# Block sums of the down projections chained by DMA, their issues spread out, and a stage's first weights loaded before a residual

## The reference

```python
def conv_ffn(h, w_up, w_dw, b_dw, w_down):
    u = depthwise_conv(h @ w_up, w_dw) + b_dw
    gate, val = jnp.split(u, 2, axis=-1)
    return (jax.nn.silu(gate) * val) @ w_down
...
    for i in range(DEPTH):
        m_lat = jnp.split((jax.nn.silu(c) @ w_mod[i] + b_mod[i])[:, None, :], 6, axis=-1)
        ...
        x_lat = x_lat + m_lat[2] * rmsnorm(y_lat, g_post_mix[i])
        h = modulate(rmsnorm(x_lat, g_pre_ffn[i]), m_lat[3], m_lat[4])
        x_lat = x_lat + m_lat[5] * rmsnorm(
            conv_ffn(h, ffn_w_up[i], ffn_w_dw[i], ffn_b_dw[i], ffn_w_down[i]), g_post_ffn[i])
```

## Time and profile before

| | |
|---|---|
| median of 3 runs | 2653.39 us (2651.99 to 2656.15) |
| the profiled execution | 2649.16 us, span 2647.1 us |
| PE busy | 2469.2 us (93%), 11028 matmuls |
| DVE busy | 1907.1 us (72%) |
| ACT busy | 1261.9 us (48%) |
| POOL busy | 1065.3 us (40%) |
| POOL's DMA queue | 145.77 MB, 27.9% of the 16 engines' span |
| SP's DMA queue | 248.46 MB, 26.2% |

### The profile page before, as it was taken

How to read it: one execution, slowest core, us unless ns; L and a number is a source line. 1 busy time by engine, 2 the same in 40 slices (tenths; PEclk the granted TensorE clock), 3 DMA queues, 4 the chain that set the end, 5 groups by cost and what they waited for, 6 DMA issues and landing times.

```text
span 2647.1 us, 32056 instructions
## 1 busy us (share of the span) xinstructions
PE 2469.2 (93%) x11028; PEld 1974.5 (75%) x11028; DVE 1907.1 (72%) x2537; ACT 1261.9 (48%) x2062; POOL 1065.3 (40%) x765
## 2 busy tenths in 40 slices
PE   8989998979899999988999799999899999889997
PEld 4878887768687787767788587657677787667886
DVE  5467675657558999865655679997479999566556
ACT  3356564546544555444554342235446555444542
POOL 0077667773034566644101221111435665542002
PEclk9999998989999999998999899999899999899999
DMA  6057666753521565454975456666414555458755
GB/s 253 26 162 174 158 162 151 188 155 83 187 96 68 148 172 154 123 125 106 271 232 175 141 155 136 127 142 148 123 53 146 160 150 151 100 125 237 244 175 175
DMA packets 170645, 400.93 MB, mean 151 GB/s; under 512 B 14977, under 2 KB 16257, under 8 KB 170497
## 3 DMA queue, kind: packets, MB, share of 16 engines
q0 software_dynamic: 59040, 145.77, 27.9%
q1 hardware_dynamic: 109872, 248.46, 26.2%
q10 hardware_dynamic: 1584, 4.85, 0.5%
HBM read 331.91 MB, written 170.92 MB: 190 GB/s over the span
## 4 chain that ended last, share of the span: by engine, by line
PE 35%; DVE 20%; DMA 18%; POOL 13%; issue 11%; ACT 2%; SPq 0%; POOLq 0%; ACTq 0%; DVEq 0%
DMA weight_sums<-units 14%; PE psum L2259 10%; PE psum L2261 10%; PE psum L2260 10%; DVE weights_f32r L1980 8%; POOL low L885 3%; DMA set<-mod_w 2%; POOL set L833 2%; DVE low L1957 2%; DVE low L1949 2%; DVE low L1947 2%; DMA low<-units 1%; POOL set L832 1%; PE psum L2475 1%; POOL low L858 1%
## 5 line engine op out<-in xcount | busy, mean ns | idle before, releaser
L2259 PE MATMUL psum<-acts_f32r,weights_f32r 128*128 128x512 f32 x1536 | 615.2, 401 | 31.7 <-ACT low L1215 9.4
L2260 PE MATMUL psum<-acts_f32r,weights_f32r 128*128 128x512 f32 x1536 | 604.3, 393 | 0.0
L2261 PE MATMUL psum<-acts_f32r,weights_f32r 128*128 128x512 f32 x1536 | 603.7, 393 | 0.0
L958 ACT ACTIVATE weights_f32r<-low 128x512 fp32r<-128x512 f32 (+2 forms) x471 | 307.6, 659 | 405.2 <-POOL low L885 173.4
L1980 DVE TENSOR_TENSOR weights_f32r<-low,weights_f32r 128x512 fp32r<-128x512 f32 x264 | 355.9, 1379 | 96.8 <-ACT weights_f32r L958 95.0
L2259 PEld LDWEIGHTS psum<-acts_f32r,weights_f32r 128*128 128x128 f32 x1536 | 292.6, 190 | 100.2 <-issue 20.9
L2261 PEld LDWEIGHTS psum<-acts_f32r,weights_f32r 128*128 128x128 f32 x1536 | 292.4, 190 | 62.8
L2260 PEld LDWEIGHTS psum<-acts_f32r,weights_f32r 128*128 128x128 f32 x1536 | 292.6, 190 | 61.1 <-issue 2.2
L858 POOL TENSOR_TENSOR low<-low 128x512 f32<-128x512 f32 x91 | 134.8, 1483 | 493.9 <-ACT low L1197 487.6
L2259 PE MATMUL psum<-high_f32r,weights_f32r 128*128 128x512 f32 (+1 forms) x485 | 204.9, 423 | 72.9 <-ACT low L958 59.8
L885 POOL TENSOR_TENSOR low<-low 128x512 f32<-128x512 f32 x150 | 253.2, 1688 | 39.8 <-DVE acts_f32r L1965 29.3
(11 more groups left out here) (253 smaller groups left out, 4969.6 us busy)
## 6 DMA issues: line engine op xcount, KB each, us to landing
low<-units SPq DMA_DIRECT2D x130, 512.0 KB, 5.8
set<-mod_w POOLq DMA_DIRECT2D x80, 512.0 KB, 4.5
weight_sums<-units POOLq DMA_DIRECT2D x44, 768.0 KB, 8.9
low<-gated_sums SPq DMA_DIRECT2D x110, 256.0 KB, 4.8
weight_sums<-units POOLq DMA_DIRECT2D x22, 1024.0 KB, 7.3
gated_sums<-low SPq DMA_DIRECT2D x22, 1024.0 KB, 4.3
low<-weight_sums SPq DMA_DIRECT2D x88, 256.0 KB, 4.2
gated_sums<-gated_sums POOLq DMA_DIRECT2D x22, 768.0 KB, 7.3
```

The costliest lines, as they stand in the source:

```text
L958: return act.activation(out, in_, ACT.Copy, scale=scale)
L2259: pe.matmul(out, wl, xh, start=first, stop=False, skip_group_check=continued)
L2260: pe.matmul(out, wh, xl, start=False, stop=False, skip_group_check=continued)
L2261: return pe.matmul(out, wh, xh, start=False, stop=last, skip_group_check=continued)
```

## The change

Three things are changed.

1. **Weight sums.** A chain takes the place of the separate sums: two copies fill four places (one quarter to two places, two quarters to one each), two accumulates make the first two sums, and two more make the third and fourth sum, each by adding the sum before it. Four half blocks are accumulated for a block where seven were. Blocks go in groups: six groups of two in layer 0 (the last of one), in layer 1 three groups of four (the last of three). So layer 0 has 24 parts with 36 DMAs, one part after every third step of POOL's loop; layer 1 has 12 parts with 18 DMAs in a row. `DOWN` is renumbered to the new places; its products keep their order.
2. **Gated sums.** The first accumulate goes onto two places where it went onto three, and the one of rounds `p` >= 11 too. The third (onto one place) adds the second's sum, and it stands in the next round, behind L923's addition. SP stores three copies of a gated half where it stored four.
3. **SP's order.** The four `pw1` loads stand before the wait for `t_lo` and the residual.

```diff
-DOWN = (("W", 0, "B", 0), ("W", 1, "G", 0), ("S", 1, "T", 2), ("S", 0, "T", 4), ("W", 2, "T", 3), ("S", 3, "T", 1), ("S", 2, "G", 1))
+DOWN = (("W", 0, "B", 0), ("W", 1, "G", 0), ("S", 2, "T", 2), ("S", 0, "T", 3), ("W", 2, "T", 4), ("S", 1, "T", 1), ("S", 3, "G", 1))
...
+W_GROUPS = (tuple((m, min(m + 2, KB)) for m in range(0, KB, 2)), tuple((m, min(m + 4, KB)) for m in range(0, KB, 4)))
...
                 if b == 1:
+                    for q in range(4):
+                        sp.wait_ge(w_lo, W_FFN[0] + 139 + min(ITEMS, ITEMS - 2 + q))
+                        sp.wait_ge(g_lo, min(ITEMS, ITEMS - 2 + q))
+                        load_unit("pw1", q, U_PW1 + q)
                     sp.wait_ge(t_lo, T_BASE[1, 0] + CB)
...
             ffn(0, 1)
-            for q in range(4):
-                sp.wait_ge(w_lo, W_FFN[0] + 139 + min(ITEMS, ITEMS - 2 + q))
-                sp.wait_ge(g_lo, min(ITEMS, ITEMS - 2 + q))
-                load_unit("pw1", q, U_PW1 + q)
...
                 if part == 0:
-                    pool.dma_start(sums, units[base][:, HALF:L].unsqueeze(1).to_broadcast([P, 4, HALF])).then_inc(summed, 16)
+                    pool.dma_start(sums[:, 0:2], a21.unsqueeze(1).to_broadcast([rows, 2, HALF])).then_inc(summed, 16)
+                    pool.dma_start(sums[:, 2:4], blocks[:, :, :, 0:HALF].rearrange("k m p n -> (m p) k n")).then_inc(summed, 16)
                 if part == 1:
-                    pool.dma_start(sums[:, 0:3], units[base][:, 0:HALF].unsqueeze(1).to_broadcast([P, 3, HALF]),
-                                   accum_op=ADD, max_dma_last_dim=4 * HALF).then_inc(summed, 16)
-                if part == 2:
-                    pool.dma_start(sums[:, 1:4], units[base + KB][:, HALF:L].unsqueeze(1).to_broadcast([P, 3, HALF]),
-                                   accum_op=ADD, max_dma_last_dim=4 * HALF).then_inc(summed, 16)
-                if part == 3:
-                    pool.dma_start(sums[:, 2], units[base + KB][:, 0:HALF], accum_op=ADD, max_dma_last_dim=4 * HALF).then_inc(summed, 16)
+                    pool.dma_start(sums[:, 0], a11, accum_op=ADD, max_dma_last_dim=4 * HALF).then_inc(summed, 16)
+                    pool.dma_start(sums[:, 1], a22, accum_op=ADD, max_dma_last_dim=4 * HALF).then_inc(summed, 16)
+                if part > 1:
+                    pool.dma_start(sums[:, part], sums[:, part - 1], accum_op=ADD, max_dma_last_dim=4 * HALF).then_inc(summed, 16)
...
-                    for n in range(4 * KB * (t * CB + k) // (10 * CB), 4 * KB * (t * CB + k + 1) // (10 * CB)):
-                        weight_sum(0, n)
+                    if (t * CB + k) % 3 == 2 and t * CB + k < 72:
+                        weight_sum(0, (t * CB + k) // 3)
...
+            def second_sum(layer, j):
+
+                pool.wait_ge(g_out, 16 * (FB * layer + KB + j + 1))
+                pool.wait_ge(summed, gated_summed(layer, KB + 2 * j))
+                pool.dma_start(t_d[layer][j, 2:4].rearrange("i p n -> p i n"), g_d[layer][j][:, HALF:L].unsqueeze(1).to_broadcast([P, 2, HALF]),
+                               accum_op=ADD, max_dma_last_dim=4 * HALF).then_inc(summed, 16)
+
+            def third_sum(layer, j):
+
+                pool.wait_ge(n_out, 16 * (FB * layer + KB + j + 1))
+                pool.wait_ge(summed, gated_summed(layer, KB + 2 * j + 1))
+                pool.dma_start(t_d[layer][j, 4], t_d[layer][j, 2], accum_op=ADD, max_dma_last_dim=4 * HALF).then_inc(summed, 16)
...
                     pool.tensor_tensor(f(S_6, HALF), f(S_1, HALF), f(S_6, HALF), ADD).then_inc(u_new, 1)
+                    if p > KB:
+                        third_sum(layer, p - 1 - KB)
...
-                    gated_sum(layer, p)
-                for j in range(MAIN, FB):
-                    gated_sum(layer, j)
+                    if p < KB:
+                        first_sum(layer, p)
+                    else:
+                        second_sum(layer, p - KB)
+                third_sum(layer, MAIN - 1 - KB)
+                for j in range(MAIN - KB, KB):
+                    second_sum(layer, j)
+                    third_sum(layer, j)
```

43 lines of the change are left out of this document (20 added, 23 removed).

## The result

The changed kernel takes 2516.6 us (2511.9 to 2522.2), the kernel before, timed beside it, 2652.7. The first is the median of three executions; a fourth took 4929.2 us, far outside, and is left out (with it the median would be 2519.4). The ratio is 0.949, with a 95% interval of 0.946 to 0.953. The forecast was 2558 (2530 to 2592): the direction held, the size did not. The profiled execution has a span of 2510.0 us against 2647.1, so it gained 137.1 where the sum of the prediction was 95.

The account below looks back on a forecast made before the run. The prediction took POOL, busy 40%, to set the end in places, as it sits in front of DMAs. Terms of 59, 2, 15, 12 and 7 made 95 us; from the median of 2653.39 that gave 2558 us (2530 to 2592).

Parts of the forecast that it names:

- Attention: Layer 0's weight sums, spaced 17 us apart, shorten PE's stands for conditioning vectors: 7 us gained, bounds 26 and -19.
- 5 or 6 us come back as new waits: Attention: `mod_w` loads wait behind four pairs of DMAs on the same queue, at 1 to 2 us each.
- the first (few waits to lose) stays: Attention: PE's first stand for conditioning vectors, 5.31 us, remains; only the second falls, from 12.1 to about 7.
- the slow stretches of the clock: Attention: PE's slow stretch gets shorter, adding 2 us; an estimated 8 in the upper bound.
- Gated sums: Up projection: moving POOL's wait brings eight late rounds to 19.6 us each; 31 and 28 us by layer, 59 together.
- PE's own floor: Up projection: PE's round of 19.1 us, not counted on; it would give 4 us more per layer.
- Down projection: Start of the down projection, DMA-bound: last sums shrink by a quarter; 2 us in all, per layer up to 5 or -3.
- Layer 1's weight sums: Behind the convolution: chain of 212 us against 329 ends before ACT asks for squares, wait goes whole; 15 us (11 to 19).
- `pw1`: Between the layers: units loaded ahead let PE start 9.7 us earlier, with 0 to 6 us from the clock; 12 us.
- DVE isn't the bound late: Rival, late up projection rounds: 19.1 us each, 2550 us; with both stands of attention gone as well, 2531; 12%.
- The pairs don't starve the vectors: Denies the attention rival that each pair costs 5 us, PE's stands grow to about 17 and 19, 2584 us; 10%.
- the second sum isn't late: Denies the late-round rival that the accumulate takes 14 us, POOL and DVE wait 2 us a round, 2590 us; 9%.

Follow-up runs that it names:

- its seven variants: The seven experiments that alter only weight sums or `pw1` loads of the changed kernel; measured 1.6 to 45.3 us over it.
- the two runs with less work: Changed kernel with half the columns left out, of DVE's product of gate and value (2498.9 us) or of POOL's up projection weight sums (2501.6 us).

## Why the prediction was wrong

*Attention, 7 against 30.6: the term that failed, in three of its steps.* First, "a few DMA issues" and waits of 10.7 us were the gain, and "5 or 6 us come back as new waits", since pairs of DMAs would hold up `mod_w`. They didn't come. Over the same three vectors POOL took 139.8 us before (from 433.87) and 120.3 now (from 425.27). This is what it waited for there, before and then after:

```profile
POOL set L830 <- DMA set<-mod_w: 15.4, 2, 8.5
POOL low L830 <- DMA set<-mod_w: 4.7, 1, 4.7
POOL set L832 <- DMA set<-mod_w: 1.1, 2, 0.6
```

```profile
POOL set L834 <- DMA set<-mod_w: 8.0, 2, 5.3
POOL low L834 <- DMA set<-mod_w: 4.4, 1, 4.4
POOL set L836 <- DMA set<-mod_w: 2.4, 2, 1.7
```

Of these, 6.88 and 5.25 us lie just ahead of the stretch, at its first operation. That leaves 14.3 and 9.6 us: 4.8 us less, beside the 10.7 for the sums and 3.9 less of POOL's busy time, which makes up the 19.5. With 19.5 us less, PE's stand of 12.1 goes altogether. The loads' part is a matter of this stretch: over all of attention (140 to 700 us) POOL waited 45.7 us for `mod_w` before and 47.2 now, and 31.9 and 0 us for sums. Second, "the first (few waits to lose) stays": those waits for sums came to 31.9 us over the whole of attention, not to the 10.7 of one stretch, and the first stand went as well. Third, the slow stretches of the clock, which I took at 2 us and bounded by 8, were worth 11.9, the busy time that PE lost. Even my upper bound of 26 was under the 30.6. What the experiments show in place of my account is that the chain alone gives most of the term, 24 to 27 us at the old pace and in single blocks: it takes 34.3 us of waits for the sums down to 6.5.

*Gated sums, 59 against 68.8 (35.9 and 32.8).* The mechanism was right: no wait, a landing inside 12.3 us (7.0 in the median, even under my lower bound of 7.4), DVE as the next bound by POOL's contention, rounds of 19.5. The size was off where I gave all eight late rounds the early length. The last two take 17.7 us, some 4 us less per layer in all. That is also less than the 19.04 that every round takes where PE is the bound, the last two included; so "PE's own floor" of 19.1 was no floor for the distance between two of DVE's additions. POOL makes no more sums from 1183 us on, and I read the two short rounds as DVE, which had trailed PE, catching up with it; no run tests that. The rest, some 1 us per layer, are early rounds of 19.50 for 19.59, which I had put at nothing beside a DVE that is the bound.

*Down projection, 2 against 8.6.* The bounds were 5 and -3 per layer, and I took a value near the middle. The measured 4.3 is near the upper one, but with the scatter of this stage only layer 0's is clear (212.2 us before, 207.4 to 210.1 in the changed kernel and its seven variants), so part of the 8.6 is chance. My reason, sums smaller by a quarter, is not borne out by any run; the cause stays open.

*Layer 1's weight sums, 15 against 15.4.* The step was right, the chain ends long before ACT asks. That the number fits so well is partly luck: the trace of before that I read had the shortest wait of four, and by the run with the old sums the term is worth 22. The chain itself took 161 us to its last landing and not 212: the two accumulates of a part, issued 0.7 us apart, had both landed after 14 to 17 us, where my sum of single landings counts 23.8. The rule of the Trainium skill that I set aside (DMA: Bandwidth & Descriptors, Anatomy of one DMA) I put at some 110; with its estimate of 4.4 us per 1 MB my own sum comes to 97. The measured chain lies between. As 315 us were free, none of it mattered.

*`pw1`, 12 against 13.8.* Right: PE's stand is 3.5 us, near the 3 of the forecast, and the run with late loads gives 12.0 net.

Of the rivals, "DVE isn't the bound late" came nearest in time (2531 with both stands gone), and both stands did go; but its first half is refuted, DVE is the bound, as the two runs with less work show. That the total came near is luck. The pairs don't starve the vectors, and the second sum isn't late.

## What to carry over

Whoever changes DMAs on a queue should count the waits of everything behind them on that queue, not only of the operations that wait for those DMAs: here they were a quarter of POOL's gain over three vectors, and a kernel with large, well-spaced sums lost 45 us by them without ever waiting for a sum. A DMA whose result is awaited costs next to nothing if the wait can move behind work that lasts longer than its landing; its size then hardly matters (0.1 us a round here). And a stage's gain in a single trace means something only beside the scatter of that stage in kernels that share its code. Where two engines contend for SBUF, work moved onto the busier one can shorten it.

## What the runs showed of the hardware

- Large DMAs inside HBM hold up the loads behind them on their queue: with copies of 2 MB and accumulates of 1.5 MB (13.8 and 14.5 us to landing in the median) the 512 KB loads behind them held POOL up for 117.9 us, with copies of 512 KB and accumulates of 256 KB for 30.7 us.
- A DVE subtraction of 128x512 took 1646 ns in the mean with 13.0 us of POOL's work in a round of 19.5, 1034 with the sums halved, 846 with three additions taken from POOL, and 675 to 679 at its shortest and in the median of that last kernel.
- In attention the slow clock cost 11.9 us of PE's busy time beside stands of 17.0. From 574 us, behind the stand of 12.1 us, PE was busy at 0.50 for 8 us and at 0.87 for the next 8.
